# Probabilities times values of two heads, issued in turn into the two column halves of the array

## The chip, the cores and the metric

The kernel runs on one core of a Trainium2 chip. The metric is the device time of one execution in microseconds (us). The core has five engines that run their own instruction lists and wait for each other by semaphores: TensorE (PE) multiplies matrices into PSUM, VectorE (DVE) and ScalarE (ACT) work on PSUM and SBUF, GpSimd (POOL) does small things and starts one kind of DMA, SyncE (SP) starts the others. The matrix array is 128 rows (the contracted index) by 128 columns (the output partitions).

## The reference, cut to what matters

Two layers of a first block and one layer of a second block, on 512 rows of width 1024 (plus 16 meta rows in the first block), all in float32.

```python
# first block, layers l = 0 and 1
proj = einsum('bld,de->ble', h, w_in[l])            # a, g, zc, q, k, v, za, qi, ki, wi
y_conv = conformer_conv_branch(...)                 # 31 taps, layer norm, gate
idx = top_k(index scores, 132)                      # the keys that a query may see
s = q . k / 8, masked to idx and to the past        # 8 heads of 64
p = softmax(s);  y_attn = (p @ v) * silu(za)
h = layer_norm(ALPHA * h + concat(y_conv, y_attn) @ w_out[l])
# second block
attn = softmax(q . k / 8) @ v * silu(gate_a)        # 8 query heads of 64, 2 value heads, all 512 keys
gm = gelu(u) * spatial_mix(vv) * silu(gate_b)
y = sigmoid(g0) * (attn @ Wa) + sigmoid(g1) * (gm @ Wb)
x = rmsnorm(x + y @ w_out)
```

The change is at `p @ v` of both.

## The kernel before

Every engine's program is written out in order. A use of a PSUM buffer is marked on a semaphore when it is full (`psum_full`) and when it has been taken (`act_took`, `dve_took`); `claim` makes PE wait until the last use of a bank was taken.

Attention goes item by item. An item is one tile of 128 queries (tile 0: the 16 meta rows) and one head. Layer 0 has 40 items (tiles 0 to 4, eight heads each), layer 1 has 32 (tiles 1 to 4), the second block 32 (four tiles). Tile t of the first block sees 16 + 128 t keys. An item passes these steps in the first block:

- PE `attention_logits` (L1219): logits of an even head and the next odd one, the one on rows 0 to 63 of the array, the other on rows 64 to 127, into PSUM C and D.
- DVE `masked_logits` (L1697): adds the mask and finds the maximum.
- ACT `exps` (L721): exponential with its sum.
- DVE `normalise` (L1704, L1706): reciprocal of the sum, product.
- PE `turn_probs` (L1252, L1257): transposes the probabilities into PSUM A; the part of the meta keys, in tile 4, into B.
- ACT `take_probs_t` (L735, L738, L739): copies them to `pt[i % 2]`, two buffers.
- PE `probs_times_v` (L1268, L1271): values times probabilities. The weights are 64 columns of `v`, so the output is 64 partitions of PSUM B: the lower 64 for an even head, the upper 64 for an odd one. The first matmul contracts the 16 meta keys, the others 128 keys each.

Each engine has extra operations that are woven between the items by `attention_extras`: on PE `todo[i]` holds halves of gate projections (L1163, 24 matmuls), transposes of the convolution there and back (L1282, L1291) and output rows (L1313, 24 matmuls); on ACT tanh of the gates, the splitting of weights (L605, L606), the affine step (L759) and others; on DVE the taps of the convolution, gates, statistics, residuals and norms. ACT's order in an item is: `exps(i + 1)`, `take_probs_t(i)`, its `todo[i]`. DVE's is: `normalise(i)`, `masked_logits(i + 2)`, its `todo[i]`. PE's, before, is: for even i `attention_logits(i + 2)`; `todo[i]`; `turn_probs(i)`; `probs_times_v(i - 1)`.

In layer 0 PE's `todo` is empty for the even items 4, 10, 20, 32 and 34 and for the odd items 9, 11, 15, 17, 21, 27, 29, 31, 35, 37 and 39; in layer 1 for the even items 4, 14, 18, 24, 28 and 30 and for the odd items 15, 17, 21 and 23.

The second block does the same with `logits2` (L1485, L1486), `max2` (L2023), `exps2` (L919, three buffers), `normalise2` (L2029, L2031), `turn_probs2` (L1495), `take_probs2_t` (L929) and `probs_times_v2` (L1504, four matmuls). Every second item it also computes a column tile of the merge gates (`merge_gate`, L1163, 24 matmuls, into the second bank of B), which ACT takes with tanh (L896) in `take_gates`; behind that, for every second gate, ACT splits a block of weights in two halves over two items (L605, L606). In the first eight items the rows of the other branch are turned as well: `turn_mlp` on PE (L1476), `part_hi("gm", ...)` on ACT (L936), `mlp_low` on DVE (L2015).

## Time and profile before

| what | us |
|---|---|
| three runs | 1138.95, 1141.35, 1142.75 (median 1141.35) |
| the profiled execution | 1140.32 |
| its span, first to last instruction | 1138.5 |
| PE busy in the span | 1069.5 (94%) |
| DVE busy | 696.3 (61%) |
| ACT busy | 579.9 (51%) |

By the chain of work that ended last, attention of layer 0 lies at about 190 to 372 us, that of layer 1 at about 575 to 726, and that of the second block at 881 to 1043. A matmul's duration includes the time in which it leaves the array, so matmuls in a row overlap in the profile: the distance of their starts is what one costs. A float32 matmul of `probs_times_v`, of the logits shows as two records, and has two weight loads; the float32 transposes and the projections (with operands split in two parts) show as one.

### The profile page before, as it was taken

Reading aid. Unit: us, or ns where it says so; the run is one execution under the profiler, and the core shown is the slowest. Engines: PE = TensorE matmul, PEld = TensorE weight load, DVE = VectorE, ACT = ScalarE, POOL = GpSimd, SP = SyncE. Lnnn points to the kernel's source line nnn. Section 1 sums busy time; section 2 is a strip of 40 time slices with the busy share of each in tenths; the row PEclk is TensorE's granted clock in tenths of the full one; section 3 lists DMA queues with packets and bytes.
Section 4 is the critical chain, followed back from the end, with each engine's and each line's share of the span. In section 5 each row is a group of like instructions: output and inputs, shape, how many; then the busy total and the mean of one; then the engine's idle time right before and its main releaser. Section 6 shows DMA issues by size and latency. Waiting matters only on the chain.

```text
span 1138.5 us, 16658 instructions
## 1 busy us (share of the span) xinstructions
PE 1069.5 (94%) x6484; PEld 900.7 (79%) x6484; DVE 696.3 (61%) x1553; ACT 579.9 (51%) x938; POOL 129.7 (11%) x185
## 2 busy tenths in 40 slices
PE   7998999889999899889999899969999999999997
PEld 7987898857767799789888567858888777778885
DVE  3999999965554569999989554634631332232422
ACT  6574871637333548478255643444565464554331
POOL 0000100002110100010011211223200000000001
PEclk9998999989989999999999899979999999999999
DMA  8785773735101768458546520484777525344761
GB/s 283 174 186 166 163 170 96 171 63 127 49 1 37 185 134 214 118 113 196 136 115 146 112 86 1 148 199 134 176 176 207 144 75 129 94 104 119 168 165 74
DMA packets 23822, 152.36 MB, mean 134 GB/s; under 512 B 2865, under 2 KB 3377, under 8 KB 6849
## 3 DMA queue, kind: packets, MB, share of 16 engines
q0 software_dynamic: 9648, 68.75, 32.6%
q1 hardware_dynamic: 14096, 82.55, 19.8%
q8 instruction: 52, 0.85, 0.3%
q14 instruction: 26, 0.20, 0.1%
HBM read 149.20 MB, written 2.10 MB: 133 GB/s over the span
## 4 chain that ended last, share of the span: by engine, by line
PE 81%; ACT 7%; DMA 5%; DVE 4%; issue 2%; POOL 0%; POOLq 0%; SPq 0%; DVEq 0%; ACTq 0%
PE psum_B L1163 19%; PE psum_A L1163 13%; PE psum_B L1196 9%; PE psum_A L1196 8%; PE psum_A L1313 6%; PE psum_B L1271 3%; DMA w_lo<-in_weights 3%; PE psum_C L1219 3%; PE psum_B L1504 3%; PE psum_B L1313 2%; PE psum_A L1517 2%; DMA w_raw<-in_weights 2%; DVE conv_acc L1600 2%; PE psum_B L1517 2%; ACT w_hi L605 2%
## 5 line engine op out<-in xcount | busy, mean ns | idle before, releaser
L1600 DVE SCALAR_TENSOR_TENSOR conv_acc<-u,vec,conv_acc 128x528 f32<-128x528 f32 (+1 forms) x240 | 172.9, 756 | 3.2
L1163 PE MATMUL psum_B<-x_hi,w_hi 128*128 128x264 f32 (+3 forms) x512 | 145.4, 323 | 8.2 <-ACT shifted L660 5.6
L1163 PE MATMUL psum_B<-x_lo,w_hi 128*128 128x264 f32 (+3 forms) x512 | 143.1, 318 | 0.0
L1163 PE MATMUL psum_B<-x_hi,w_lo 128*128 128x264 f32 (+3 forms) x512 | 142.8, 317 | 0.0
L998 POOL DMA_DIRECT2D w_lo<-in_weights x67 | 60.9, 909 | 685.8 <-ACT w_lo L606 685.8
L605 ACT ACTIVATE w_hi<-w_raw 128x2048 fp32r<-128x2048 f32 (+2 forms) x87 | 129.9, 1493 | 14.8 <-DMA w_raw<-in_weights 14.5
L606 ACT ACTIVATE w_lo<-w_raw 128x2048 fp32r<-128x2048 f32 (+2 forms) x87 | 129.3, 1486 | 0.0
L1163 PE MATMUL psum_A<-x_hi,w_hi 128*128 128x264 f32 (+2 forms) x496 | 117.9, 295 | 7.2 <-DMA w_lo<-in_weights 3.3
L1163 PE MATMUL psum_A<-x_lo,w_hi 128*128 128x264 f32 (+2 forms) x496 | 115.4, 290 | 0.0
L1163 PE MATMUL psum_A<-x_hi,w_lo 128*128 128x264 f32 (+2 forms) x496 | 115.3, 290 | 0.0
L1163 PEld LDWEIGHTS psum_B<-x_hi,w_hi 128*128 128x128 f32 (+1 forms) x512 | 89.3, 190 | 19.2 <-issue 12.5
L1163 PEld LDWEIGHTS psum_B<-x_lo,w_hi 128*128 128x128 f32 (+1 forms) x512 | 89.0, 189 | 6.2
L1163 PEld LDWEIGHTS psum_B<-x_hi,w_lo 128*128 128x128 f32 (+1 forms) x512 | 88.9, 189 | 6.2
L1163 PEld LDWEIGHTS psum_A<-x_hi,w_hi 128*128 128x128 f32 x496 | 83.4, 192 | 11.6 <-issue 4.0
L1163 PEld LDWEIGHTS psum_A<-x_lo,w_hi 128*128 128x128 f32 x496 | 83.3, 192 | 0.8
L1163 PEld LDWEIGHTS psum_A<-x_hi,w_lo 128*128 128x128 f32 x496 | 83.2, 192 | 0.7
L735 ACT ACTIVATE probs_t<-psum_A 128x256 f32<-128x256 f32 (+2 forms) x48 | 23.3, 486 | 93.2 <-PE psum_A L1257 93.1
L1655 DVE MATCH_REPLACE8 score<-top,score 128x528 f32<-128x528 f32 (+3 forms) x136 | 65.5, 492 | 0.0
L1196 PE MATMUL psum_B<-w_hi,x_hi 128*128 128x512 f32 (+1 forms) x160 | 62.2, 389 | 3.2 <-issue 3.2
L1196 PE MATMUL psum_B<-w_hi,x_lo 128*128 128x512 f32 (+1 forms) x160 | 62.1, 388 | 0.0
L1196 PE MATMUL psum_B<-w_lo,x_hi 128*128 128x512 f32 (+1 forms) x160 | 61.8, 386 | 0.0
L1646 DVE MAX8 top<-score 128x8 f32<-128x528 f32 (+3 forms) x136 | 58.9, 494 | 0.0
(323 smaller groups left out, 2234.7 us busy)
## 6 DMA issues: line engine op xcount, KB each, us to landing
w_raw<-in_weights SPq DMA_DIRECT2D x67, 1024.0 KB, 5.7
w_lo<-in_weights POOLq DMA_DIRECT2D x65, 1024.0 KB, 8.8
x_first<-in_x_t SPq DMA_DIRECT2D x4, 528.0 KB, 7.0
h<-in_x SPq DMA_DIRECT2D x1, 2048.0 KB, 9.7
out<-h SPq DMA_DIRECT2D x4, 512.0 KB, 2.6
post_ln_g<-in_post_ln_g SPq DMA_DIRECT2D x2, 512.0 KB, 3.9
post_ln_b<-in_post_ln_b SPq DMA_DIRECT2D x2, 512.0 KB, 5.6
w_raw<-in_weights SPq DMA_DIRECT2D x2, 288.0 KB, 5.4
```

Source lines behind the costliest of these rows:

```text
L605: act.activation(whi[n % RING][:, a:b], raw[n % RING][:, a:b], ACT.Copy)
L606: got = act.activation(wlo[n % RING][:, a:b], raw[n % RING][:, a:b], ACT.Copy, scale=-1.0)
L998: pool.dma_start(wlo[n % RING][:, 0:width], io["weights"][n, :, 0:width], accum_op=ALU.add) \
L1163: mm = pe.matmul(ps[0:cols, i, 0:b - a], w[wp][:, kt, at:at + cols], x[xp][:, kt, a:b], start=(kt == 0 and wp + xp == 0), stop=(kt == KD - ...
L1196: mm = pe.matmul(ps[:, 0, 0:width], act_parts[xp][:, kt, c0:c0 + P], w[wp][:, kk, at:at + width], start=(kt == 0 and wp + xp == 0), stop=( ...
L1219: mm = pe.matmul(banks[odd][0:SIZE[t], i, 0:b - a], qs[s:s + HD, hd // 2, START[t]:END[t]], ks_of[s:s + HD, a:b], start=True, stop=True)
L1271: mm = pe.matmul(out, v[:, j, hd * HD:hd * HD + HD], src[:, (j - 1) * P:(j - 1) * P + n], start=False, stop=(j == t))
L1313: mm = pe.matmul(ps, x[xp][:, kt, START[t]:START[t] + P], w[wp][:, kk, 0:DC], start=(kt == 0 and wp + xp == 0), stop=(kt == KD - 1 and wp ...
L1517: mm = pe.matmul(ps[:, 0, :], w[wp][:, kt, d % 4 * P:d % 4 * P + P], parts[xp][:, kt, :], start=(kt == 0 and wp + xp == 0), stop=(kt == CT ...
L1600: got = dve.scalar_tensor_tensor(dst, src, w, dst, ALU.mult, ALU.add)
L1646: dve.max(top8[:, t - 1, :], vals).then_inc(topk_max.mark((l, r, t)), 1)
L1655: dve.match_replace(vals, top8[:, t - 1, :], vals, MARK).then_inc(topk_marked.mark((l, r, t)), 1)
```

## The change

`probs_times_v` and `probs_times_v2` now treat two heads in one call: for each tile of keys first the even head's matmul into partitions 0 to 63, then the odd head's into 64 to 127. They need both copies of the probabilities, so PE's order around them is new.

- First block, per pair: the next logits go ahead of `turn_probs(i)` if `todo[i]` has work, otherwise behind it; `todo[i]` comes behind `turn_probs(i)`, and `todo[i + 1]` behind `turn_probs(i + 1)`; then the pair's product. ACT, DVE, POOL and SP keep their order.
- Second block, per pair: `turn_probs2(i)`, `turn_probs2(i + 1)`, a merge gate, two logits, the product, and `turn_mlp` behind it. Gate 0 stands ahead of the loop. ACT takes the gate in the odd item, where it was the even one; `part_hi("gm", ...)` and `mlp_low` move from the odd items 1 to 7 to the even items 2 to 8.

```diff
@@ ACT, second block
-                if i % 2 and i < 8:
-                    part_hi("gm", i // 2)
                 take_probs2_t(i)
-                if i % 2 == 0:
+                if i % 2 == 0 and 2 <= i <= 8:
+                    part_hi("gm", i // 2 - 1)
+                if i % 2:
                     take_gates("gm", i // 2)
                     waiting += [(m, half) for m in SPLIT_AT.get((2, "gm", i // 2), []) for half in range(2)]
@@ PE, first block
             def probs_times_v(l, i):
...
+                pe.wait_ge(act_took.sem, act_took.at((l, "PT", t, hd + 1)))
+                for j in [0] + list(range(1, t + 1)):
+                    for odd in range(2):
+                        s, col = HD * odd, (hd + odd) * HD
+                        src = pt[odd]
+                        if j == 0:
+                            keys, probs = v[0:META, 0, col:col + HD], src[0:META, t * P:t * P + n]
+                        else:
+                            keys, probs = v[:, j, col:col + HD], src[:, (j - 1) * P:(j - 1) * P + n]
+                        mm = pe.matmul(ps[s:s + HD, 0, hd // 2 * P:hd // 2 * P + n], keys, probs,
+                                       start=(j == 0), stop=(j == t))
...
+                for i in range(0, n, 2):
+                    if todo[i] and i + 2 < n:
+                        attention_logits(l, i + 2)
                     turn_probs(l, i)
-                    if i:
-                        probs_times_v(l, i - 1)
-                probs_times_v(l, n - 1)
+                    if not todo[i] and i + 2 < n:
+                        attention_logits(l, i + 2)
+                    woven(i)
+                    turn_probs(l, i + 1)
+                    woven(i + 1)
+                    probs_times_v(l, i)
@@ PE, second block
                 for j in range(4):
-                    mm = pe.matmul(ps[s:s + HD, 0, hd // 2 * P:hd // 2 * P + P], v2[:, j, g * HD:g * HD + HD],
-                                   pt2[i % 2][:, j * P:j * P + P], start=(j == 0), stop=(j == 3))
+                    for odd in range(2):
+                        s = HD * odd
+                        mm = pe.matmul(ps[s:s + HD, 0, hd // 2 * P:hd // 2 * P + P], v2[:, j, g * HD:g * HD + HD],
+                                       pt2[odd][:, j * P:j * P + P], start=(j == 0), stop=(j == 3))
...
+            merge_gate(0)
+            for i in range(0, n, 2):
+                turn_probs2(i)
+                turn_probs2(i + 1)
+                if i:
                     merge_gate(i // 2)
+                if i + 4 < n:
+                    logits2(i + 4)
+                    logits2(i + 5)
+                probs_times_v2(i)
+                if i < 8:
+                    turn_mlp(i // 2)
@@ DVE, second block
-                if i % 2 and i < 8:
-                    mlp_low(i // 2)
+                if i % 2 == 0 and 2 <= i <= 8:
+                    mlp_low(i // 2 - 1)
```

PE in layer 0 at items 34 and 35 (tile 4, nothing woven in), before. `exps2`, `exps3` are the two items' probabilities; `probs_t1` is still that of item 33. The logits are those of 36 and 37.

```order
L1252 MATMUL psum_A<-ident_64,exps2_121 128x128 x4
L1257 MATMUL psum_B<-ident_64,exps2_121 16x128
L1268 MATMUL psum_B<-probs_t1_114,v_103 64x128
L1271 MATMUL psum_B<-probs_t1_114,v_103 64x128 x4
L1252 MATMUL psum_A<-ident_64,exps3_122 128x128 x4
L1257 MATMUL psum_B<-ident_64,exps3_122 16x128
L1268 MATMUL psum_B<-probs_t0_113,v_103 64x128
L1271 MATMUL psum_B<-probs_t0_113,v_103 64x128 x4
L1219 MATMUL psum_C<-k_97,q_88 128x264
L1219 MATMUL psum_D<-k_97,q_88 128x264
```

The same place in the changed kernel, down to the second pair of matmuls of the product.

```order
L1252 MATMUL psum_A<-ident_64,exps2_121 128x128 x4
L1257 MATMUL psum_B<-ident_64,exps2_121 16x128
L1219 MATMUL psum_C<-k_97,q_88 128x264
L1219 MATMUL psum_D<-k_97,q_88 128x264
L1219 MATMUL psum_C<-k_97,q_88 128x264
L1219 MATMUL psum_D<-k_97,q_88 128x264
L1252 MATMUL psum_A<-ident_64,exps3_122 128x128 x4
L1257 MATMUL psum_B<-ident_64,exps3_122 16x128
L1274 MATMUL psum_B<-probs_t0_113,v_103 64x128
L1274 MATMUL psum_B<-probs_t1_114,v_103 64x128
```

The logits moved between the two transposes, and no product stands between a transpose and the next one; the product of items 34 and 35 follows the second transpose directly.

PE in the second block between gates 2 and 3, before: items 4 and 5 with the products of 3 and 4.

```order
L1495 MATMUL psum_A<-ident_64,exps2_1_144 128x128 x4
L1504 MATMUL psum_B<-probs2_t1_147,v2_130 64x128 x4
L1485 MATMUL psum_C<-k2_hi_131,q2_first_151 128x512
L1486 MATMUL psum_C<-k2_lo_172,q2_first_151 128x512
L1476 MATMUL psum_B<-ident_64,u_gated_154 128x128 x4
L1495 MATMUL psum_A<-ident_64,exps2_2_145 128x128 x4
L1504 MATMUL psum_B<-probs2_t0_146,v2_130 64x128 x4
L1485 MATMUL psum_C<-k2_hi_131,q2_first_151 128x512
L1486 MATMUL psum_C<-k2_lo_172,q2_first_151 128x512
L1163 MATMUL psum_B<-x_hi_61,w_hi2_51 128x512
```

In the changed kernel, between gates 1 and 2 (the last matmuls of the product of items 2 and 3, the turn of the other branch, the transposes of items 4 and 5, the first matmul of gate 2):

```order
L1514 MATMUL psum_B<-probs2_t0_146,v2_130 64x128
L1514 MATMUL psum_B<-probs2_t1_147,v2_130 64x128
L1484 MATMUL psum_B<-ident_64,u_gated_154 128x128 x4
L1503 MATMUL psum_A<-ident_64,exps2_1_144 128x128 x4
L1503 MATMUL psum_A<-ident_64,exps2_2_145 128x128 x4
L1163 MATMUL psum_B<-x_hi_61,w_hi2_51 128x512
```

The two transposes now stand side by side, directly ahead of the gate, and nothing is left on PE between the first and the second.

ACT in the second block, changed kernel, from the take of gate 0 on. It shows what stands between a gate's tanh and the exponential that the next pair's second transpose needs (`exps_0`, item 3), and that the copy of item 2 (`probs_t_146`) stands ahead of `mlp_hi`.

```order
L896 ACTIVATE merge_tanh<-psum_B,b_merge_half 128x512
L605 ACTIVATE w_hi_49<-w_raw_53 128x1024
L606 ACTIVATE w_lo_57<-w_raw_53 128x1024
L919 ACTIVATE exps_0_143,prob_sums<-psum_D,neg_max 128x512
L929 ACTIVATE probs_t_146<-psum_A 128x512
L936 ACTIVATE mlp_hi<-psum_B 128x4x128
```

Before, the gate was taken one item earlier, and `mlp_hi` stood ahead of the copy.

## Rows read from the trace of the kernel before

**Rows 1.** Busy time by stretch: us, then PE, PEld, DVE, ACT, POOL, clock, DMA.
```profile
245.00:372.00 127.00, 122.64 (x709) 90.83 (x708) 62.06 (x156) 55.86 (x136) 19.19 (x27) 0.97 0.19 50
945.00:1043.00 98.00, 98.00 (x530) 78.09 (x528) 26.05 (x61) 50.30 (x91) 5.47 (x5) 1.00 0.43 109
```
**Rows 2.** Timeline of PE, layer 0, tile 4: start us, duration us, engine, line, operation.
```profile
355.84 0.27 PE L1257 MATMUL psum_B<-ident,exps 128*16 128x128 f32 x1
356.05 0.43 PE L1268 MATMUL psum_B<-probs_t,v 16*64 16x128 f32 x2
356.40 1.09 PE L1271 MATMUL psum_B<-probs_t,v 128*64 128x128 f32 x8
357.42 0.55 PE L1252 MATMUL psum_A<-ident,exps 128*128 128x128 f32 x3
```
**Rows 3.** Timeline of PE, logits of two heads in two row halves.
```profile
316.33 0.49 PE L1219 MATMUL psum_C<-k,q 64*128 64x264 f32 x1
316.34 0.49 PE L1219 MATMUL psum_D<-k,q 64*128 64x264 f32 x1
```
**Rows 4.** The chain that ended last, two gates of block 2: start, length, what.
```profile
946.52 5.56 PE psum_B L1163 x24
956.32 5.56 PE psum_B L1163 x24
```
**Rows 5.** Timeline of ACT in block 2, from a copy of probabilities on.
```profile
911.36 0.60 ACT L929 ACTIVATE probs_t<-psum_A 128x512 f32<-128x512 f32 x1 [6.36 <-PE psum_A L1495]
911.85 0.68 ACT L896 ACTIVATE merge_tanh<-psum_B,b_merge_half 128x512 f32<-128x512 f32 x1
912.42 1.06 ACT L605 ACTIVATE w_hi<-w_raw 128x1024 fp32r<-128x1024 f32 x1
913.37 1.05 ACT L606 ACTIVATE w_lo<-w_raw 128x1024 fp32r<-128x1024 f32 x1
914.31 0.69 ACT L919 ACTIVATE exps<-psum_D,neg_max 128x512 f32<-128x512 f32 x1
914.88 0.21 ACT L919 ACTIVATION_READ_ACCUMULATOR exps<-psum_D,neg_max 128x1 f32 x1
914.97 0.60 ACT L936 ACTIVATE mlp_hi<-psum_B 128x512 fp32r<-128x512 f32 x1
```
**Rows 6.** Timeline of DVE, same place.
```profile
915.61 0.69 DVE L2015 TENSOR_TENSOR mlp_lo<-psum_B,mlp_hi 128x512 fp32r<-128x512 f32 x1 [8.66 <-ACT mlp_hi L936]
...
916.41 0.49 DVE L2031 TENSOR_SCALAR exps<-exps,prob_rsums 128x512 f32<-128x512 f32 x1
```
**Rows 7.** Timeline of DVE, layer 0, items 34 and 35.
```profile
343.82 0.71 DVE L1697 CUSTOM_DVE_ANT_0 exps<-psum_C,mask 128x528 f32<-128x528 f32 x1 [6.42 <-PE psum_D L1219]
...
344.45 0.68 DVE L1758 SCALAR_TENSOR_TENSOR h<-h,psum_A 128x512 f32<-128x512 f32 x1
...
345.96 0.49 DVE L1706 TENSOR_SCALAR exps<-exps,prob_rsums 128x528 f32<-128x528 f32 x1
```
**Rows 8.** Timeline of ACT, layer 0, item 34.
```profile
344.52 0.60 ACT L738 ACTIVATE probs_t<-psum_A 128x512 f32<-128x512 f32 x1 [1.18 <-PE psum_B L1257]
345.01 0.25 ACT L739 ACTIVATE probs_t<-psum_B 16x128 f32<-16x128 f32 x1
```
**Rows 9.** Timeline of PE, end of the transpose of item 17, layer 0.
```profile
261.68 0.27 PE L1257 MATMUL psum_A<-ident,exps 128*16 128x128 f32 x1
```
**Rows 10.** Timeline of ACT, item 16 and the copy of item 17, layer 0.
```profile
260.79 0.49 ACT L735 ACTIVATE probs_t<-psum_A 128x384 f32<-128x384 f32 x1 [4.90 <-PE psum_A L1257]
...
265.17 0.47 ACT L735 ACTIVATE probs_t<-psum_A 128x384 f32<-128x384 f32 x1
```
**Rows 11.** Timeline of PE, item 32 of layer 0, with its idle time and releaser.
```profile
330.04 0.63 PE L1252 MATMUL psum_A<-ident,exps 128*128 128x128 f32 x4 [2.36 <-DVE exps L1706]
```
**Rows 12.** The chain that ended last, output rows at two times.
```profile
332.86 7.91 PE psum_A L1313 x24
349.80 5.77 PE psum_A L1313 x24
```
**Rows 13.** Busy time and granted clock (first of the last three numbers) by stretch.
```profile
330.00:337.00 7.00, 6.96 (x23) 5.26 (x24) 5.13 (x12) 1.46 (x4) 0.80 (x2) 0.55 0.01 2
```

More of the change, by code:

```diff
@@ L926, in take_probs2_t @@
                 if i >= 2:
-                    act.wait_ge(psum_full.sem, psum_full.at((2, "PV2", *items2[i - 2])))
+                    act.wait_ge(psum_full.sem, psum_full.at((2, "PV2", *items2[i - i % 2 - 1])))
                 act.activation(pt2[i % 2][:, :], ps[:, 0, :], ACT.Copy).then_inc(act_took.mark(use), 1)
@@ L1263, in probs_times_v @@
                 ps = claim(use, "B", (0,)) if hd == 0 else bank["B"]
-                pe.wait_ge(act_took.sem, act_took.at((l, "PT", t, hd)))
-                s = HD * (hd % 2)
-                out = ps[s:s + HD, 0, hd // 2 * P:hd // 2 * P + n]
-                src = pt[i % 2]
-                mm = pe.matmul(out, v[0:META, 0, hd * HD:hd * HD + HD], src[0:META, t * P:t * P + n],
-                               start=True, stop=(t == 0))
-                for j in range(1, t + 1):
-                    mm = pe.matmul(out, v[:, j, hd * HD:hd * HD + HD], src[:, (j - 1) * P:(j - 1) * P + n],
-                                   start=False, stop=(j == t))
-                if hd == HEADS - 1:
+                pe.wait_ge(act_took.sem, act_took.at((l, "PT", t, hd + 1)))
[9 more added lines that the diff above has]
+                                       start=(j == 0), stop=(j == t))
+                if hd == HEADS - 2:
                     mm.then_inc(psum_full.mark(use), 1)
@@ L1408, in _, with woven @@
                     pe.wait_ge(rope_made.sem, rope_made.at((l, "k", c)))
-                attention_logits(l, 0)
-                for i in range(n):
-                    if i % 2 == 0 and i + 2 < n:
-                        attention_logits(l, i + 2)
+                def woven(i):
                     for op in todo[i]:
@@ L1423, in _ @@
                             output_conv(l, *op[1:])
+                attention_logits(l, 0)
+                for i in range(0, n, 2):
+                    if todo[i] and i + 2 < n:
+                        attention_logits(l, i + 2)
                     turn_probs(l, i)
[L1425 to L1427 removed]
+                    if not todo[i] and i + 2 < n:
[4 more added lines that the diff above has]
+                    probs_times_v(l, i)
                 turn["AB"] = 1
@@ L1500, in probs_times_v2 @@
                 ps = claim((2, "O2", t), "B", (0,)) if hd == 0 else bank["B"]
-                pe.wait_ge(act_took.sem, act_took.at((2, "PT2", t, hd)))
-                s, g = HD * (hd % 2), hd // 4
+                pe.wait_ge(act_took.sem, act_took.at((2, "PT2", t, hd + 1)))
+                g = hd // 4
                 for j in range(4):
-                    mm = pe.matmul(ps[s:s + HD, 0, hd // 2 * P:hd // 2 * P + P], v2[:, j, g * HD:g * HD + HD],
-                                   pt2[i % 2][:, j * P:j * P + P], start=(j == 0), stop=(j == 3))
-                mm.then_inc(psum_full.mark((2, "PV2", t, hd)), 1)
+                    for odd in range(2):
+                        s = HD * odd
+                        mm = pe.matmul(ps[s:s + HD, 0, hd // 2 * P:hd // 2 * P + P], v2[:, j, g * HD:g * HD + HD],
+                                       pt2[odd][:, j * P:j * P + P], start=(j == 0), stop=(j == 3))
+                mm.then_inc(psum_full.mark((2, "PV2", t, hd + 1)), 1)
             def branch(name, d, buf=None):
@@ L1538, in _ @@
             n = len(items2)
-            for i in range(3):
+            for i in range(4):
                 logits2(i)
-            for i in range(n):
-                if i + 3 < n:
-                    logits2(i + 3)
-                if i % 2 == 0:
-                    merge_gate(i // 2)
-                if i % 2 and i < 8:
+            merge_gate(0)
[3 more added lines that the diff above has]
+                if i:
+                    merge_gate(i // 2)
+                if i + 4 < n:
[3 more added lines that the diff above has]
+                if i < 8:
                     turn_mlp(i // 2)
-                turn_probs2(i)
-                if i:
-                    probs_times_v2(i - 1)
-            probs_times_v2(n - 1)
             for t in range(4):
@@ L2097, in _ @@
                     max2(i + 2)
-                if i % 2 and i < 8:
-                    mlp_low(i // 2)
+                if i % 2 == 0 and 2 <= i <= 8:
+                    mlp_low(i // 2 - 1)
                 if i > 2 and i % HEADS == 2:
```

## The prediction

> **What bounds the kernel now.** I read the stretches first: in the attention of layer 0 from 245 us on, PE is busy 122.64 of 127 us, and in the second block 98.00 of 98.00, while DVE and ACT have half their time free [rows 1]. So an instruction taken off PE shortens the run there, and a wait put onto PE lengthens it. Before 245 us (and in the first items of layer 1) DVE with the taps is as full as PE. Next I read the timelines around one product and around one copy, to price what is removed and what is newly waited for.
>
> **What is removed on PE.** For tile 4 the product of one head takes, from the last transpose (355.84) to the next one (357.42), 1.58 us, less 0.11 for that transpose's own slot: 1.47 [rows 2]. It has ten records, two of 16 keys and eight of 128. The eight start within 1.02 us and so cost 0.11 each and some 0.14 once; the array also pauses at each change of shape: 0.21 from transpose to first matmul, where 0.11 is a slot, and 0.35 over two records of 16 keys, where two slots are 0.22. Each key tile less takes two records away, so I take 1.47, 1.25, 1.03 and 0.81 for tiles 4 to 1, and 0.2 for tile 0.
> The trace before has no two matmuls in two column halves. The nearest row is that of the row halves: the logits of C and D start 0.01 us apart and run beside each other [rows 3]. I take the same for the column halves: a pair of heads then costs what one did. Lower bound of the gain: no overlap at all, and only the changes of shape saved. Four pairs per tile: layer 0 saves 4 x (1.47 + 1.25 + 1.03 + 0.81 + 0.2) = 19.0, layer 1 saves 18.2, the second block 16 x 1.1 (eight records, 1.02, and one pause of 0.09) = 17.6. Together 54.9 us of PE work.
>
> The Trainium skill (TensorE: Matmul & The Clock Gate, "Measured speedup vs the span model") gives 2.38 times for three column tiles, which would be about 1.6 for two; by an estimate from that figure a step of two costs 0.14 instead of 0.11, 360 steps cost some 10 us more, and the sum below would be about 1165. No run so far shows it here.
>
> **What is newly waited for, second block.** Gates start 9.80 us apart in the steady part, and one takes 5.56 [rows 4]. In the new order nothing stands on PE between the two transposes of a pair, and the second needs the normalised item i + 1. Its exponential is behind the tanh of the gate on ACT's list, and behind a half split of weights for every second gate. Count from the slot behind the gate's last matmul. PE: two logits 0.93, product 1.1, first transpose 0.44, so it is ready for the second at 2.47. ACT and DVE, from the starts and durations of [rows 5, 6]: gate out and tanh begins 0.20; next begins 0.57 later (0.77); split 0.95 + 0.94 (2.66); exponential and sum 0.57 + 0.21 (3.44); reciprocal and product 0.19 + 0.49 and two hand-overs of 0.04 (4.2). Without a split it is 2.3, which PE covers. So a pair takes 5.56 + 2.47 + 0.44 = 8.5 us without a split, and 10.2 with one. A pair that also writes the attention's upper part (items 9, 17, 25, ACT 0.48 more) takes 10.7. Against 9.80 that is -1.3 for gates 5, 7, 9, 11, 13, +0.4 for 6, 10, 14 and +0.9 for 4, 8, 12.
> For items 2, 4, 6 and 8 there is a round trip: DVE has `mlp_low` between the two normalisations, it waits for `mlp_hi`, and ACT has that behind the copy of item i, which waits for the first transpose. From its end: copy 0.48 to the next start, `mlp_hi` 0.60, `mlp_lo` 0.61 to the reciprocal, 0.68, with hand-overs about 2.7 us in which PE has nothing [rows 5, 6]. Before, two such pairs lost about 1 us each to `mlp_low` and the others none. This gives about 11.7 per gate interval for gates 1 to 3 and 13.8 for gate 0 (a first split, and the product waits for its copies), some 3 + 2.5 us more than before. At the end, behind gate 15, one product stands where two transposes and three products stood: -2.9. Sum of the second block: -6.5 + 3.9 + 3.1 + 2.5 - 2.9 = about 0: waits of 18 us eat the 17.6.
>
> **First block.** Three new waits.
> (a) Where `todo[i]` is empty for even i, the logits come behind the first transpose, but DVE has their masking ahead of `normalise(i + 1)`, for which the second transpose waits. From the logits' end, tile 4: hand-over 0.2, masking 0.71, normalise 0.15 + 0.49, 0.1: 1.7, plus whatever DVE has in between, a residual for example 1.3 (0.68 twice) [rows 7]. Item 34 is such a place.
> (b) The product waits for the copy of its odd head. After the transpose: 0.2, 0.60, 0.25 partly over it, 0.05, less the pause that is there anyhow: 0.9 in tile 4, 0.5 in tile 1, at each odd item with empty `todo` [rows 8].
> (c) ACT has that copy behind its own extras of item i. At item 16 the transpose of 17 ends at 261.95 and its copy starts at 265.17, behind tanh, affine steps and a split that follow the copy at 260.79 [rows 9, 10]. Before, a gate projection covered it; now the product stands there and waits about 4 us.
> Net by pair, wait less saving, layer 0: 12: 0; 14: +0.5; 16: +2.6; 18, 20: -0.3, -0.2; 22: +0.9 (the transpose of 23 is now ahead of its output rows and waits for its exponential); 24: -1.3; 26, 28, 30: -0.5 each; 32: +0.4; 34: +2.1; 36, 38: -0.6 each: together +2. Items 0 to 11: DVE is full, and at items 4 and 10 it now waits for logits: +1.5. Layer 1: items 0 to 11 -2; then +1.7, 0, +0.7, +0.8, -0.5, +1.2, +0.3, -1.5, +1.6, +0.4 for pairs 12 to 30: +2.7. First block +6.2: of 37.2 saved nothing is left. Each entry is good to about 1 us. If all waits were a third smaller the block would come out at -8, a third larger at +20.
>
> **The clock.** Behind the idle 2.36 us at 330.04 [rows 11] the granted clock was 0.55 over 7 us, its lower level, 1.2 GHz, for most of that [rows 13], and 24 matmuls took 7.91 where they take 5.77 [rows 12]: 2.1 us for one fall. The new order makes some 20 waits of 1.5 to 4 us (ten in the second block, which had full clock). If half of them bring a fall and each costs 1 to 2.1 us, for part of it lies in waits, that is 10 to 20; four falls are there already. I take +10, bounds 0 and +30.
>
> **Sum.** The profiled execution took 1140.3 (span 1138.5 and 1.8 around it), 1.0 under the median of the runs. 1140.3 - 54.9 + 18 (block 2) + 43.4 (first block) + 10 (clock) = 1156.8, say 1157.
>
> **Rivals.**
> A, the waits are half of what I count. ACT and DVE are free for half the time [rows 1]; if they run ahead, the second transpose and the copy come early. Place: the second transpose of each pair in the second block and (a) and (b) in the first. It decides for faster when the 61 us of waits fall below some 50. With half of them and no more clock falls: 1140.3 - 54.9 + 31 = 1116. Against it: ACT's and DVE's lists are fixed, and the chain through tanh, split and exponential is made of rows, not of load.
> B, the column halves don't run beside each other. Then 464 records in the first block give back 232 slots of 0.11, 25 us, and the second block 128 slots, 14, of which 5 lie in waits for splits: 1157 + 34 = 1191. For it: no row shows column halves; against it: the row halves do run so.
> C, gains and losses cancel, 1137.9 to 1143.7 (0.3% to either side, about what a measurement of this kernel can tell from no change).
> D, the clock falls at nearly every new wait: +20 more, 1177.
>
> The Trainium skill (TensorEngine Tiling (Array Packing), "PSUM Bottleneck") warns that tiling speeds up TensorE and not the copies out of PSUM, which may bound next. That is the forecast's mechanism, here as latency rather than load; by that rule alone the second block would gain nothing and the layers little, and the time would lie between C and the forecast.
>
> **Chances.** Forecast 45% (own range 1144 to 1172), A 23%, B 15%, C 9%, D 8%. Faster by over 0.3%: 0.23; within: 0.09; slower: 0.68. The range takes most of A and B in: 1112 to 1188.
>
> **What would show it.** Right: in the timeline of PE the even and the odd product start 0.01 us apart and a pair of tile 4 takes about 1.5 us; idle time ahead of the transposes of block 2, released by DVE's normalisation, about 2.7 us four times and 1.7 six times; gates 8.5 and 10.2 us apart in turn; idle ahead of the products, released by ACT's copies, above all at item 16 of layer 0; more stretches with a clock of 0.5. Wrong: second transposes without idle time (A), products 0.11 apart one after the other (B), a clock of 1.0 throughout the second block.

## The result

| | us |
|---|---|
| before, median of 4 runs | 1140.46 |
| changed, median of 4 runs (1182.39 to 1190.28) | 1185.19 |
| ratio | 1.0395, 95% interval 1.0349 to 1.0442 |
| profiled execution of the changed kernel | 1182.39, span 1180.6 |
| forecast | 1157 (1112 to 1188) |

Slower, as forecast, but by 44.7 us where the forecast had 16.7.

I cut both traces at the first and the last product of each attention. These are the three stretches before, each line one stretch: us, then busy time of PE, PEld, DVE, ACT and POOL with their counts, then the granted clock of PE, the DMA share and GB/s.

```profile
204.00:368.00 164.00, 150.63 (x910) 114.31 (x909) 99.00 (x253) 74.37 (x188) 21.71 (x31) 0.94 0.32 78
584.00:720.00 136.00, 129.93 (x810) 98.03 (x809) 88.59 (x209) 71.55 (x163) 20.43 (x29) 0.96 0.41 100
892.00:1043.00 151.00, 149.02 (x803) 118.40 (x802) 42.37 (x98) 79.04 (x144) 8.71 (x8) 1.00 0.41 102
```

The same three stretches of the changed kernel:

```profile
204.00:379.00 175.00, 140.27 (x907) 108.44 (x906) 100.10 (x254) 75.52 (x187) 21.89 (x31) 0.86 0.29 70
595.00:755.00 160.00, 124.83 (x809) 95.84 (x806) 87.28 (x208) 71.85 (x160) 20.56 (x29) 0.84 0.34 82
923.00:1085.00 162.00, 138.48 (x804) 109.89 (x804) 43.12 (x97) 79.69 (x143) 8.49 (x8) 0.95 0.40 97
```

Each line gives two numbers by subtraction: idle time of PE (length less busy) and how much busy time fell. Idle time went from 13.4, 6.1 and 2.0 to 34.7, 35.2 and 23.5: +72.0 us. Busy time fell by 10.4, 5.1 and 10.5, 26.0 in all, where 54.9 us of work should have gone: the other 28.9 us are work done at the lower clock, and the clock column says so (0.94, 0.96, 1.00 to 0.86, 0.84, 0.95). 72.0 - 26.0 = +46.0; the rest of the span is 4 us shorter.

The 28.9 rests on the forecast's 54.9. The granted clock gives the price a second time, without it. These are the sums over all pieces of the three stretches in which it is at its lower level, 1.2 GHz (us, then busy time of the same engines, then the means), first before, then changed:

```profile
sum 30.72, PE 26.45 PEld 18.71 DVE 20.21 ACT 13.32 POOL 2.93; mean PE 5.29 PEld 3.74 DVE 4.04 ACT 2.66 POOL 0.59
sum 116.05, PE 89.97 PEld 66.12 DVE 53.96 ACT 51.64 POOL 18.69; mean PE 5.62 PEld 4.13 DVE 3.37 ACT 3.23 POOL 1.17
```

There are five pieces before and sixteen in the changed kernel, and PE is busy in them for 63.5 us more. Matmuls of a gate start 0.43 us apart there and 0.23 at full clock, so nearly half of that time is the clock's: 29 us by this ratio, 32 if it were all half (an estimate). The busy time then confirms the saving too: 26.0 + 29 is 55.

Who released PE, in the changed kernel: us in total, times, longest.

```profile
PE psum_A L1252 <- DVE exps L1717: 43.2, 18, 5.3
PE psum_A L1503 <- DVE exps L2042: 23.4, 10, 3.3
PE psum_B L1274 <- ACT probs_t L735: 18.6, 15, 3.5
PE psum_A L1257 <- DVE exps L1717: 6.1, 6, 3.7
```

Before, the first of these was:

```profile
PE psum_A L1252 <- DVE exps L1706: 12.0, 10, 2.6
```

Two kinds of wait, as forecast: second transposes for a normalisation, products for a copy. The timeline of PE in tile 4, answering to [rows 2], shows the pair's product. Columns: start, duration, engine, line, operation, in brackets idle time and releaser.

```profile
371.02 1.46 PE L1274 MATMUL psum_B<-probs_t,v 16*64 16x128 f32 x20 [0.83 <-ACT probs_t L739]
```

Twenty records of two heads take 1.46 us, as long as one head's ten did. The column halves run side by side, and the wait of 0.83 is (b) of the forecast (0.9).

The second block's chain of waits, answering to [rows 4]: start, length, what.

```profile
929.15 7.14 PE psum_B L1163 x24
942.47 5.57 PE psum_B L1163 x24
954.83 6.61 PE psum_B L1163 x24
967.85 6.92 PE psum_B L1163 x24
980.05 5.56 PE psum_B L1163 x24
988.57 5.57 PE psum_B L1163 x24
998.90 5.58 PE psum_B L1163 x24
1007.44 5.57 PE psum_B L1163 x24
```

From 980.05 on the gates start 8.52, 10.33, 8.54 apart (forecast 8.5 and 10.2; one with the attention's part is 10.85 for 10.7). By the starts of their first matmuls the first ones, from gate 0 at 914.98 on, are 13.9, 13.3, 12.3, 13.0 and 12.3 apart, where the forecast had 13.8, 11.7, 11.7, 11.7 and 10.7, and here gates of 7.14, 6.61 and 6.92 us stand where one takes 5.57 at full clock.

### The profile page after: what moved, and what is told of

It is laid out like the page before. It is cut to its first block, busy times and chain, and to the rows that moved or that the text cites. A ratio compares the mean times of both kernels' runs of the same rounds, so it can differ in the third digit from the quotient of the medians.

```text
span 1180.6 us, 16658 instructions
## 1 busy us (share of the span) xinstructions
PE 1044.0 (88%) x6484; PEld 883.9 (75%) x6484; DVE 698.7 (59%) x1553; ACT 582.7 (49%) x938; POOL 129.5 (11%) x185
## 4 chain that ended last, share of the span: by engine, by line
PE 77%; DVE 10%; ACT 7%; issue 3%; DMA 3%; POOL 0%; POOLq 0%; DVEq 0%; SPq 0%; ACTq 0%
PE psum_B L1163 19%; PE psum_A L1163 13%; PE psum_B L1196 9%; PE psum_A L1196 8%; PE psum_A L1316 6%; DVE conv_acc L1611 4%; PE psum_C L1219 4%; PE psum_B L1274 3%; PE psum_A L1252 2%; PE psum_B L1316 2%; PE psum_A L1527 2%; PE psum_B L1527 2%; DMA w_raw<-in_weights 1%; ACT w_hi L605 1%; PE psum_A L1503 1%
## 5 line engine op out<-in xcount | busy, mean ns | idle before, releaser
L1163 PE MATMUL psum_B<-x_hi,w_hi 128*128 128x264 f32 (+3 forms) x512 | 150.2, 332 | 7.4 <-ACT shifted L660 6.2
L1163 PE MATMUL psum_B<-x_lo,w_hi 128*128 128x264 f32 (+3 forms) x512 | 146.6, 325 | 0.0
L1163 PE MATMUL psum_B<-x_hi,w_lo 128*128 128x264 f32 (+3 forms) x512 | 146.1, 324 | 0.0
L605 ACT ACTIVATE w_hi<-w_raw 128x2048 fp32r<-128x2048 f32 (+2 forms) x87 | 129.7, 1490 | 13.0 <-DMA w_raw<-in_weights 12.6
L1163 PEld LDWEIGHTS psum_B<-x_hi,w_hi 128*128 128x128 f32 (+1 forms) x512 | 92.3, 196 | 15.3 <-issue 8.4
L1163 PEld LDWEIGHTS psum_B<-x_hi,w_lo 128*128 128x128 f32 (+1 forms) x512 | 91.5, 194 | 6.8
L1163 PEld LDWEIGHTS psum_B<-x_lo,w_hi 128*128 128x128 f32 (+1 forms) x512 | 91.9, 195 | 6.2
L1252 PE MATMUL psum_A<-ident,exps 128*128 128x128 f32 x160 | 35.5, 327 | 43.2 <-DVE exps L1717 43.2
L1708 DVE CUSTOM_DVE_ANT_0 exps<-psum_C,mask 128x144 f32<-128x144 f32 (+4 forms) x36 | 16.9, 469 | 89.1 <-PE psum_D L1219 89.1
L1252 PEld LDWEIGHTS psum_A<-ident,exps 128*128 128x128 f32 x160 | 20.9, 160 | 63.4 <-issue 61.8
L1274 PE MATMUL psum_B<-probs_t,v 128*64 128x128 f32 (+2 forms) x464 | 43.4, 316 | 21.2 <-ACT probs_t L735 18.6
```

Of the source, the lines that this page charges most:

```text
L605: act.activation(whi[n % RING][:, a:b], raw[n % RING][:, a:b], ACT.Copy)
L1163: mm = pe.matmul(ps[0:cols, i, 0:b - a], w[wp][:, kt, at:at + cols], x[xp][:, kt, a:b], start=(kt == 0 and wp + xp == 0), stop=(kt == KD - ...
L1252: pe.transpose(main[:, 0, (j - 1) * P:(j - 1) * P + n], src[0:n, START[j]:END[j]], ident[0:n, 0:n])
L1274: mm = pe.matmul(ps[s:s + HD, 0, hd // 2 * P:hd // 2 * P + n], keys, probs, start=(j == 0), stop=(j == t))
```

## The experiments

Ratios are against runs of the kernel before on the same chip.

**One block at a time.** The first block as before, only the second changed.

> Only the second block is changed; the first block stands as before. In the trace of the changed kernel the second block's attention is 11.0 us longer than before (162.1 against 151.1 us from the first product to the last), with 21.4 us more idle time on PE and 17 us at the lower clock where there were none. Theory (each block carries its own loss, the two don't touch each other): 1140 + 8 to 11 = about 1150. Rival (the second block's loss is inherited, its weights or its clock being late because the first block was disturbed): no loss, 1140 or faster, and no stretch at a clock of 0.5 in the second block.

Measured 1151.1 (ratio 1.009, 1.006 to 1.0121). From its first to its last product the second block took 163.4 us with 23.4 idle; the changed kernel 162.1 and 23.4. The loss is made in the block itself: about 10 us of the 45 are the second block's, and by subtraction 35 the first's. The idle 23.4 us repeat to 0.1 in every kernel with this second block, but the clock varies: layer 1, unchanged here, took 131.6 us at full clock where the profile before has 136.1 at 0.96. So a difference of 4 or 5 us between single profiles of a stretch can be the clock's chance alone.

**The overlap alone.** Within each pair, all of the even head's matmuls first:

```diff
-                for j in [0] + list(range(1, t + 1)):
-                    for odd in range(2):
+                for odd in range(2):
+                    for j in [0] + list(range(1, t + 1)):
```

The second block's two loops are swapped in the same way.

> The changed kernel with the same order, but within a pair the even head's matmuls all stand ahead of the odd head's, so nothing can run in two column halves at once. This prices the overlap alone. Theory (the overlap is real and the product lies on the path of nearly every pair in the first block, while in the second the pairs that wait anyway swallow it): the first block loses 232 slots of 0.11, 25 us, the second the 6 pairs without a wait, 5 us: 1185 + 30 = 1215, and each pair of tile 4 takes about 2.4 us from first to last start instead of 1.2. Rival (waits for the copies and normalisations set the pace, so the product's length hardly counts): under 10 us slower, 1190 to 1195.

Measured 1219.0 (1.0702, 1.0661 to 1.0743), 34 us above the changed kernel. A pair of tile 4:

```profile
358.36 2.82 PE L1274 MATMUL psum_B<-probs_t,v 16*64 16x128 f32 x20
```

2.82 against 1.46: the overlap gives 1.36 per pair of tile 4. Layer 0's stretch is 12.6 us longer, layer 1's 20.5 (some of it clock, 0.83 there), the second block's 2.0. The forecast had 25 us in the first block and 9 in the second; they came as 33 and 2, so that the sum of 34 agrees is partly luck. The overlap itself is there, and in the first block it is worth more than was counted.

**Idle time filled.** Ten transposes of a constant into the bank that the next transposes overwrite, behind `claim` and ahead of the wait (first block; in the second ahead of ten of the sixteen second transposes):

```diff
+FILL = 10
...
+                if i % 2 and not extras[l]["pe"][i - 1]:
+                    for _ in range(FILL):
+                        pe.transpose(main[:, 0, 0:P], ident[:, :], ident[:, :])
                 pe.wait_ge(probs_made.sem, probs_made.at((l, i)))
```

> The changed kernel, with ten transposes of a constant (1.1 us of array work) into the bank that the next transposes will overwrite, put ahead of the wait at the 21 places with the long waits for a normalisation: the odd item's transposes where nothing was woven into the even item (11 places in the first block) and in ten pairs of the second block. The waits themselves must not get shorter by it: the normalisation doesn't depend on PE. Theory (the idle time pulls the clock down, and this costs some 29 us: busy PE time fell by only 26 us where 55 us of work went): the stretches at 0.5 become fewer, about half of them, and the time falls by 8 to 20 us, to 1165 to 1177. Rival (the low clock comes with the pattern of work and not with the idle time, or costs next to nothing since it lies in the waits): the same share at 0.5 and 1185, or up to 10 us slower where the filler outlasts a wait.

Measured 1179.7 (1.0362, 1.0325 to 1.0398): the intervals overlap, so no gain is shown, and the 8 to 20 us expected did not come. Half of the filler in the second block stood where nothing waited. As plain matmuls, and placed right:

> The filler again, as plain matmuls of a constant (ten, 1.1 us), and in the second block now ahead of the transposes that do wait (pairs 1 to 5, 7, 9, 11, 13, 15; in the first filler kernel half of them stood at pairs without a wait, where each cost its full 1.1 us: gate intervals of 8.52 became 9.63). Theory (idle time brings the lower clock, and it costs time outside the waits): the second block has no or one stretch at 0.5 and its gate intervals 1 to 5 fall from 13.9, 13.3, 12.3, 13.0 and 12.3 to about 12 each; in all 10 to 15 us under the changed kernel, 1170 to 1175. Rival (the intervals are the chain of ACT and DVE alone): intervals as in the changed kernel, 1180 to 1185.

Measured 1160.8 (1.0213, 1.017 to 1.0255). In these two kernels `FILL` was already the name of another constant, the fill value of the index scores of future keys. So other keys are chosen and the output is wrong, though apart from that value and the filler the instructions are the same. The next two kernels use another name and split the gain.

> The changed kernel with the filler (ten matmuls of a constant, 1.1 us) only in the second block, ahead of the ten second transposes that wait. It splits what the filler in both blocks gave (24 us in the time, and in the trace 7.5 us in the second block: 154.6 instead of 162.1 between its first and last product, none of it at the lower clock). Theory (each stretch at the lower clock is made and paid where the idle time is): the second block's stage is 154 to 156 us and the rest as in the changed kernel: 1185 - 7 = 1178. Rival (a filler in one block also moves the clock elsewhere): the second block's gain is not 7 but under 3, or the first block's share changes by over 5 us.

> The same filler only in the first block, ahead of the 11 second transposes that have no woven work behind the first ones. Theory: the remaining part of the 24 us, l0 170 and l1 154.5 us between their first and last products (174.9 and 160.1 in the changed kernel), 1185 - 12 to 17 = 1168 to 1173, less time at the lower clock in both. Rival (the earlier kernel's first block gained from something else than the filler, since it also had the constant of the causal fill of the index scores changed): nothing gained, 1185.

Measured 1175.2 (1.0308, 1.029 to 1.0326) and 1174.1 (1.031, 1.0269 to 1.0352). Against 1.0395 each is about 0.9% faster, 10 us, and the two add up to about the 1.8% (21 us) of the kernel with both, whose filler in the first block is twice as long. The second block filled, in the same columns as above:

```profile
924.00:1079.00 155.00, 152.38 (x1004) 126.63 (x1004) 43.42 (x98) 79.95 (x144) 8.48 (x8) 1.00 0.40 100
```

Clock 1.00, and 155 us where it was 162. One filler, and its transposes behind it without a wait:

```profile
992.47 0.66 PE L1509 MATMUL psum_A<-ident,exps 128*128 128x128 f32 x4
992.97 2.40 PE L1506 MATMUL psum_A<-ident 128*128 128x128 f32 x20
995.20 0.60 PE L1509 MATMUL psum_A<-ident,exps 128*128 128x128 f32 x4
```

Ten matmuls are twenty records and 2.2 us (the expectation's 1.1 holds for ten transposes, which the first and the fourth of these kernels have), a little more than the shorter waits: intervals of 10.33 became 10.75. In the first block the filler covers only part of waits of up to 5 us, and the clock there stays low for 44 us even in the kernel with both fillers (before 31). So I take the filler's gain as a lower bound of the clock's price: some 20 us, where the accounting above says 28.9 and the forecast 10.

**The round trip of the second block.** DVE's `mlp_low` one item later:

```diff
-                if i % 2 == 0 and 2 <= i <= 8:
+                if i % 2 and 3 <= i <= 9:
                     mlp_low(i // 2 - 1)
```

> The changed kernel, with DVE's mlp_low of the second block one item later, behind the normalisation of the odd item instead of between the two. This takes away the round trip (first transposes, copy, mlp_hi, mlp_low, normalisation, second transposes) in four pairs. Theory (the round trip is what makes gate intervals 1 to 4 12.3 to 13.9 us where later ones are 8.5 to 10.9): the wait of the second transposes falls from 2.6 to 1.0 in four pairs, the clock stays up there, intervals 1 to 4 become 11 or less, the whole 6 to 9 us faster: 1176 to 1179. Rival (the tanh and the splits set it): under 2 us.

Measured 1179.3 (1.0371, 1.0335 to 1.0408); the second block's stretch fell from 162.1 to 157.0, and the first four intervals to 13.2, 12.3, 11.1 and 10.8. The waits of the second transposes fell from 23.4 to 15.1 us, but four of the gates now wait for `mlp_low`, 4.2 us in all, so that idle time in the block fell by only 4.0 (23.4 to 19.4). The trip is real and costs 4 us of waits; the fifth us is clock. On the whole kernel the ratios differ by 2.7 us and their intervals overlap, so the theory's 6 to 9 is not shown.

**The order in the first block.** Logits always ahead:

```diff
-                    if todo[i] and i + 2 < n:
+                    if i + 2 < n:
                         attention_logits(l, i + 2)
                     turn_probs(l, i)
-                    if not todo[i] and i + 2 < n:
-                        attention_logits(l, i + 2)
```

> The changed kernel, but in the first block the logits of the next pair always stand ahead of the even item's transposes, as before the change; where nothing is woven in they stood behind them (11 places), and there the second transposes wait 1.6 to 5.3 us, 38 us in all. Theory (DVE takes the masking of the late logits ahead of the normalisation that PE waits for): with the logits 1.5 us earlier the masking is done by then, half or more of the 38 us goes, and with it some stretches at the lower clock: faster by 15 to 25 us, 1160 to 1170. Rival (the second transposes wait for the exponential and DVE's other work anyway, and the logits behind the first transposes at least gave PE something to do): no gain or slower by up to 10 us, the idle time moves to the same transposes at full length.

Measured 1175.4 (1.0314, 1.0261 to 1.0367): 9 us, less than expected, and the intervals just overlap. The same waits are there, only shorter (layer 1: 3.5, 1.2, 3.6, 3.8, 4.6 and 2.6 us where they were 3.9, 2.0, 4.3, 4.5, 5.3 and 2.6); idle time fell by 5.5 us in the two layers. What they consist of shows on DVE in the changed kernel at items 28 and 29 of layer 1, where PE's second transposes wait until 736.19:

```profile
730.89 0.71 DVE L1708 CUSTOM_DVE_ANT_0 exps<-psum_C,mask 128x528 f32<-128x528 f32 x1 [7.69 <-PE psum_D L1219]
...
731.52 0.68 DVE L1769 SCALAR_TENSOR_TENSOR h<-h,psum_A 128x512 f32<-128x512 f32 x1
732.24 0.69 DVE L1772 BATCH_NORM_STATS2 stats<-h 128x6 f32<-128x512 f32 x1
732.85 1.27 DVE L1787 SCALAR_TENSOR_TENSOR h<-h,meanvar,post_ln_g 128x1024 f32<-128x1024 f32 x1
734.16 1.28 DVE L1791 SCALAR_TENSOR_TENSOR h<-h,rstd,post_ln_b 128x1024 f32<-128x1024 f32 x1
735.36 0.16 DVE L1715 RECIPROCAL prob_rsums<-prob_sums 128x1 f32<-128x1 f32 x1
735.55 0.50 DVE L1717 TENSOR_SCALAR exps<-exps,prob_rsums 128x528 f32<-128x528 f32 x1
```

```profile
736.19 1.09 PE L1252 MATMUL psum_A<-ident,exps 128*128 128x128 f32 x4 [5.33 <-DVE exps L1717]
```

DVE is idle for 7.69 us, waits for the logits, and only then does all its woven work of item 28 (3.8 us), ahead of the one product that PE needs. PE waits for DVE, which had waited for PE. Before, the output rows of item 29 (5.77 us) stood between the two transposes; now they stand behind. Two further kernels move that cover back. First only the odd item's woven work:

```diff
                     woven(i)
+                    woven(i + 1)
                     turn_probs(l, i + 1)
-                    woven(i + 1)
                     probs_times_v(l, i)
```

> The changed kernel, but in the first block the work woven into the odd item stands ahead of that item's transposes again, as before the change, and so between the two transposes of the pair. Theory (the long waits for normalisations, 3.7 and 2.3 us in layer 0 and 3.9, 4.3, 4.5, 5.3 and 2.6 in layer 1, arise because this cover was moved away, while DVE does its own woven work behind the late masking): these 27 us go; in return the product now follows the odd transposes directly and waits 0.7 to 0.9 us for the copy in some 21 pairs, 17 us. Net 10, with the clock up to 15 us faster than the changed kernel: 1170 to 1175. Rival (missing cover by the product is what counts, wherever the woven work stands): the idle time moves to the product in full, no gain or slower.

Measured 1173.6 (1.0292, 1.0259 to 1.0325), as expected; then all of it (logits, `woven(i)`, `turn_probs(i)`, `woven(i + 1)`, `turn_probs(i + 1)`, product):

> The changed kernel, with logits, woven work and transposes of the first block all in the order from before the change; only the product is paired and stands behind the odd item's transposes. The second block is the changed one. It differs from the kernel with the delayed product (first block 1119, second block added 11: about 1130) only in where the pair's product stands. Theory (what is left is the wait for the odd copy, 0.5 to 0.9 us at each of 36 pairs, more where ACT has a tanh or a split ahead of it, and the missing product between the transposes): 25 to 35 us slower than that: 1155 to 1165. Rival (the woven order did all the damage, the place of the product none): 1130 to 1140.

Measured 1182.7 (1.0376, 1.0337 to 1.0415): no better than the changed kernel, 20 us worse than expected. PE's waits in the one and the other:

```profile
PE psum_B L1274 <- ACT probs_t L735: 26.3, 24, 4.3
...
PE psum_A L1252 <- DVE exps L1717: 19.9, 13, 4.0
```

```profile
PE psum_B L1274 <- ACT probs_t L735: 29.4, 24, 3.9
...
PE psum_A L1252 <- DVE exps L1715: 12.8, 9, 3.1
```

The waits for normalisations go back from 43.2 to 19.9 and to 12.8, what they were before the change, but the product's own wait grows from 18.6 to 26.3 and 29.4. With two smaller lines of the same kind it is 34 and 37 us, about 1.0 for each of the 36 pairs, where my expectation had taken 0.5 to 0.9; and in the second kernel transposes wait 7.0 us more for the bank that the copies leave late. The granted clock is 0.88 in both layers. As long as the product stands directly behind its odd transposes, the order around it mostly chooses which wait is seen: in all three of these kernels the first block has 64 us of idle time, where the changed kernel has 70 and the kernel before 19.

**The product one item later.** PE's order is that of the kernel before, and the product of a pair stands behind the next item's transposes:

```diff
                     turn_probs(l, i)
-                    if i:
-                        probs_times_v(l, i - 1)
-                probs_times_v(l, n - 1)
+                    if i % 2 == 0 and i:
+                        probs_times_v(l, i - 2)
+                probs_times_v(l, n - 2)
```

The copies need a third buffer; in the first block it lies where the index weights were, in the second the later buffers move by 768 bytes. First block only, then both:

> First block only (the second stands as before the change): the same paired products in turn, but PE keeps the order from before the change, and the product of the pair i - 2, i - 1 stands behind the transposes of item i, where only the product of i - 1 stood; for this a third buffer for the copies of the probabilities. No wait for a copy or a normalisation is newly exposed behind an even item; behind an odd item the product is missing as cover. Theory (pairing itself gives 37 us in the first block, and the order around it is what costs): 1140 - 37 + at most 12 for lost cover and clock = 1103 to 1115. Rival (in the first block DVE and ACT set the pace, so that PE's saved time only turns into idle time wherever the product is put): 1130 to 1140, with 30 us more idle time on PE.

> As the run before it, and the second block in the same way: order as before the change, products in turn for the pair i - 2, i - 1 behind the transposes of item i, three buffers. Theory: 17.6 us less PE work in the second block, where DVE and ACT have half their time free and a gate interval of 9.80 us falls to 8.7: another 12 to 17 us off, 1090 to 1102 in all. Rival (the chain tanh, split, exponential, normalisation sets the interval, as it does in the changed kernel's 10.33): no gain in the intervals with a split, 5 to 8 us off.

Measured 1119.5 (0.9859, 0.9822 to 0.9896) and 1110.7 (0.9758, 0.9719 to 0.9797). The three stretches of the second of these:

```profile
208.00:358.00 150.00, 132.78 (x878) 101.68 (x877) 95.41 (x244) 71.67 (x182) 21.11 (x31) 0.91 0.33 79
579.00:701.00 122.00, 108.42 (x782) 82.83 (x781) 84.87 (x200) 68.27 (x155) 19.92 (x29) 0.97 0.42 105
886.00:1016.00 130.00, 125.58 (x768) 100.36 (x764) 39.46 (x92) 73.82 (x135) 7.60 (x7) 0.99 0.44 116
```

The stretches begin an item or two later in the program, so their lengths flatter it; idle time and clock don't. 17.2, 13.6 and 4.4 us are idle, 35.2 against 21.4 before and 93.4 in the changed kernel, and gates stand 8.61 us apart. The measured times lie 4 and 9 us above the ranges expected; of the 12 to 17 us expected from the second block 9 came, its rival's figure, though the intervals with a split fell with the others.

The first of these kernels isolates the cause in the first block. Its order on PE is that of the last kernel of the section above (logits, woven work and transposes as before the change); only the product stands elsewhere, with the third buffer that this needs, and the second block, priced alone at 0.9%, is left as before. By the ratios 1.0376 - 0.0090 - 0.9859 = 0.0427, the place of the product is worth some 49 us (within 7 by the intervals). The same paired product is faster than no pairing or slower, by where it stands.

With two buffers in the first block, the even copy waiting for the product:

> The kernel with the delayed pair products in both blocks (1110.7 us), but in the first block with the two buffers of the kernel before: the copy of an even item has to wait until the product of the last pair, which stands behind that item's transposes, has read them. Theory (the copy now starts 1 to 1.5 us later and PSUM A has one bank for the probabilities, so the odd item's transposes wait for it wherever nothing is woven between, about 17 pairs by 0.7 to 0.9 us): 12 to 18 us slower than with three buffers, 1123 to 1129. Rival (the copies have time enough, the third buffer bought nothing): within 4 us of 1111.

Measured 1123.7 (0.9861, 0.9832 to 0.989): 1.0% or 12 us behind the three buffers, with this wait of the transposes for the copy grown from 0.9 us to:

```profile
PE psum_A L1261 <- ACT probs_t L747: 5.7, 8, 0.8
```

And the delayed kernel with filler at the three longest waits of layer 0:

> The kernel with the delayed pair products in both blocks (1110.7 us), with the filler ahead of the transposes of items 10 (16 transposes of a constant, 1.8 us), 11 (10) and 32 (20, 2.2 us) of layer 0, which wait 3.3, 1.8 and 3.5 us there. Theory (the 27 us at the lower clock in layer 0 follow these waits, and two thirds of it lie beside PE work at double time): 5 to 9 us faster, 1102 to 1106, which would be the best version. Rival (the filler ends behind the wait's end, or the low clock comes from other places): 1110 to 1112.

Measured 1108.6 (0.971, 0.9677 to 0.9743). The ratio is 0.5% below the kernel without filler, but the intervals overlap: whether it helps isn't shown. Its profile has layer 0's stretch 4 us shorter, but layer 1's, which has no filler, 7 us longer. It has the lowest median, 2.9% under the kernel before.

## Why the prediction was right, and where its sizes were wrong

- **The mechanism** held. PE is the bound, the column halves run side by side, the saving of 54.9 us is real (55 by the busy time; 34 us come back when only the overlap is taken away), and newly exposed waits eat it. B falls with the product of 1.46 us, though its 1191 is the nearest figure; A falls with 72 us of waits, C with the result. D (1177, given 8%) had the right term, but for another reason: the clock did not fall at nearly every new wait. The measured time is outside the forecast's own range of 1144 to 1172, and inside the wide one only because that was widened towards A and B.
- **The step that failed is the clock**: "If half of them bring a fall and each costs 1 to 2.1 us ... I take +10". By the busy time it is 28.9, by the filler at least some 20. Of the miss of 28 us this is 10 to 19. "Half of them" was right: in the three stretches PE's waits of 1.5 us and more went from 4 to 28, and falls from 5 to 16, 11 more for the forecast's 10. What failed is the price of one, which came out at 2.6 us (28.9 by 11) where 1 was taken and 2.1 was the most allowed. There are two reasons. The 2.1 counted the 24 matmuls of [rows 12] alone, while PE was busy through all of the 7 us of [rows 13]; at nearly half of the 6.8 us at the lower level that one fall cost 3.1. And the discount "for part of it lies in waits" was too large: of the 85.3 us more at the lower level PE was busy in 63.5. In layer 1 the clock is 0.56 from 649.8 to 677.1, around waits at 652.8, 655.7, 663.2 and 668.3 of 0.6 to 4.3 us. Why some waits bring a fall and others none stays open. (The forecast's "four falls are there already" are five.) In the second block I expected falls too, and they came; its sum without them was nearly right. With the second block filled the time from the end of layer 1 to the last product is 323.0 us, before it was 322.8: the forecast's "about 0".
- **The waits**: 72.0 against 61.4. Layer 0 is right (21.4; forecast 19.0 saved and +3.5, so 22.5), the second block nearly (21.5; 18: the waits of the first pairs are 3.3, 2.6, 2.8 and 2.6 for 2.7, the other six 1.6 to 2.5 for 1.7). Layer 1 is wrong: 29.1 against 20.9. There the term (a) failed, 1.7 us "plus whatever DVE has in between": I had put in a residual, and the rows above have a residual, statistics and two passes of the post norm, 3.8 us from 731.52 to 735.36. DVE starts them only after the masking, and the masking after the late logits. Five such waits stand in layer 1, of 3.9, 2.0, 4.3, 4.5 and 5.3 us; a sixth, of 2.6, has the same passes but no logits ahead, so the order of the logits did not touch it. The forecast's entries for the pairs 14, 18, 24, 28 and 30 imply waits of 1.0, 2.1, 1.8, 3.1 and 1.9, where 2.0, 4.3, 4.5, 5.3 and 2.6 were measured: 9 us more, all of layer 1's miss.
- **(b) and (c)** were right: 0.83 for 0.9, and item 17's product waits 3.45 us at 265.0 for 4, answering to [rows 9, 10]:

```profile
268.49 1.31 PE L1274 MATMUL psum_B<-probs_t,v 16*64 16x128 f32 x8 [3.45 <-ACT probs_t L735]
```

- The round trip was priced at 11.7 us a gate and was 12.3 to 13.3; without the lower clock (second block filled) it is 11.7, 11.9 and 11.7. Here too only the clock was missing.
- The estimate worked out from the Trainium skill (TensorE: Matmul & The Clock Gate, "Measured speedup vs the span model"), some 10 us less overlap, didn't come true here: records of the two halves start together, and twenty take 1.46 us.

10.6 us of waits and 19 of clock make the miss, with the small differences in the saving and in the rest of the span. The filler shows only some 10 of the 19; for the rest the two accounts from the busy time and the granted clock agree, but no run takes the clock's falls away in the first block.

## What to carry to other kernels

Pairing two half-width products costs the distance between them: both inputs must be there before either can start. Keep the old distance by issuing the pair one item later and pay with a buffer; the same change was then worth -2.4% instead of +4%, and with two buffers in the first block -1.4%. When an order newly makes PE wait, count more than the waits: in this kernel a microsecond of new idle time cost 0.3 to 0.4 us more through the clock (20 to 29 us on 72). That ratio belongs to this kernel. To price one fall, take the busy time of the whole stretch at the lower clock, not one group of matmuls in it.

## What the hardware showed unexpectedly

In the kernel with all of the even head's matmuls ahead, the second block lost only 2 us. Its pair of sixteen records should take twice the 1.09 us of one head's eight, less what they share, and takes 1.58. Seven of the records lie in 0.60 us from 1013.17 on, where six steps of 0.11 and the 0.27 that a record takes would be 0.93:

```profile
1012.68 1.58 PE L1514 MATMUL psum_B<-probs_t,v 128*64 128x128 f32 x16
1013.17 0.60 PE L1514 MATMUL psum_B<-probs_t,v 128*64 128x128 f32 x7
```

The profile doesn't name the half of a record, but the sixteen starts fall into two rows of eight, each with one step of 0.16 and then steps of 0.11, from 1012.68 and from 1013.18 on; the first ends at 1013.50. So the odd head's matmuls began before the even head's last ones, which stand ahead of them in the program: the two column halves overlap, in part, without being issued in turn. In the first block they did not (2.82 against 1.46). There a matmul of 16 keys stands between the two heads; whether that is the reason was not tested.
